# Modulation product on TensorE inside the RWKV and attention turns, and a down projection split into high and low parts

## What is computed

```python
# first block, 256 tokens, D = 2048, D_FF = 5632
def hybrid_mixer(h, ...):                   # attention: 12 heads, RWKV: 12 heads of 64
    z = h @ w_in
    ...
    return jnp.concatenate([oa, ob, oc], axis=-1) @ w_out
def conv_ffn(h, w_up, conv_w, conv_b, w_down):
    up = h @ w_up                           # 2048 x 11264
    ...                                     # causal convolution of width 3
    return (jax.nn.gelu(gate, approximate=True) * val) @ w_down      # 5632 x 2048
# second block, two layers, on x and on a context ctx
for l in range(DEPTH_2):
    sh_l, sc_l, g_l = jnp.split(jax.nn.silu(c) @ w_mod[l] + b_mod[l], 3, axis=-1)      # w_mod[l]: 2048 x 6144
    sh_c, sc_c, g_c = jnp.split(jax.nn.silu(c_ctx) @ w_mod[l] + b_mod[l], 3, axis=-1)
    hl = xl * (1.0 + sc_l[:, None, :]) + sh_l[:, None, :]
    hc = xc * (1.0 + sc_c) + sh_c
    ...
```

## Time and profile before

| what | us |
|---|---|
| runs before: median (lowest, highest) | 3780.88 (3779.40, 3785.93) |
| span of the profiled execution | 3779.2 |
| PE busy in the span | 3340.1 (88%) |
| DVE busy | 1918.9 (51%) |
| ACT busy | 1163.8 (31%) |
| one RWKV turn (six of them) | 81.93 |
| attention, six turns | 60.51 |
| up projection, from its opening to its last matmul | 495.62 |
| from there to the last matmul of down | 308.00 |
| from there to the first matmul of the second block | 50.36 |

### The profile page before, as it was taken

The page is one execution under the profiler, slowest core; times in us unless marked ns, Lnnn a source line. Parts: engine busy times, 40 slices in busy tenths (PEclk is TensorE's granted clock), DMA queues, the critical chain, the costliest instruction groups (busy, mean ns, idle before and its releaser), DMA issues.

```text
span 3779.2 us, 47105 instructions
## 1 busy us (share of the span) xinstructions
PE 3340.1 (88%) x18040; PEld 2719.8 (72%) x18040; DVE 1918.9 (51%) x2906; ACT 1163.8 (31%) x1744; POOL 67.8 (2%) x129
## 2 busy tenths in 40 slices
PE   7988888589679999999959999999987969998977
PEld 6876666489579999988836864444446848887877
DVE  4444444455269999977762212222234354246565
ACT  3321111354345555400011223222231223245542
POOL 0000000000000000000000000000000000000000
PEclk8999998699789999999979999999998979999989
DMA  7411111134237777788852221111112204233332
GB/s 218 167 56 55 44 55 44 72 104 162 99 115 274 269 270 277 266 305 312 316 198 106 95 90 56 55 55 56 67 67 100 100 34 145 100 124 110 112 134 100
DMA packets 73108, 508.70 MB, mean 135 GB/s; under 512 B 8332, under 2 KB 8460, under 8 KB 19664
## 3 DMA queue, kind: packets, MB, share of 16 engines
q1 hardware_dynamic: 55440, 377.00, 28.0%
q0 software_dynamic: 17600, 130.75, 9.4%
HBM read 496.97 MB, written 10.75 MB: 134 GB/s over the span
## 4 chain that ended last, share of the span: by engine, by line
PE 73%; DVE 12%; DMA 7%; issue 4%; ACT 3%; DVEq 0%; ACTq 0%; SPq 0%; POOLq 0%
PE bank L544 37%; PE bank L840 10%; DMA y_f<-in_w_mod 5%; PE bank L845 5%; PE bank L596 3%; PE bank L638 2%; PE bank L495 2%; DVE x_f L1610 2%; PE bank L874 2%; PE bank L513 2%; DVE x_f L1262 1%; DVE ring_f32r L1262 1%; DMA ring_f<-in_w_in 1%; PE bank L888 1%; DVE x_f L1750 1%
## 5 line engine op out<-in xcount | busy, mean ns | idle before, releaser
L544 PE MATMUL bank<-y_f32r,high_f32r 128*128 128x256 f32 (+1 forms) x3312 | 1029.6, 311 | 56.5 <-DVE h_f32r L1262 30.2
L1262 DVE TENSOR_TENSOR ring_f32r<-ring_f,high_f32r 128x1024 fp32r<-128x1024 f32 x494 | 588.8, 1220 | 667.0 <-ACT high_f32r L946 666.4
L544 PE MATMUL bank<-y_f32r,ring_f32r 128*128 128x256 f32 (+1 forms) x2608 | 803.6, 308 | 0.0
L544 PE MATMUL bank<-h_f32r,high_f32r 128*128 128x256 f32 (+1 forms) x2432 | 743.0, 305 | 1.9 <-DVE ring_f32r L1262 1.9
L946 ACT CAST high_f32r<-ring_f 128x1024 fp32r<-128x1024 f32 x494 | 491.9, 1045 | 733.5 <-PE bank L544 609.5
L544 PEld LDWEIGHTS bank<-y_f32r,high_f32r 128*128 128x128 f32 x3312 | 636.5, 192 | 91.6 <-issue 48.0
L544 PEld LDWEIGHTS bank<-y_f32r,ring_f32r 128*128 128x128 f32 x2608 | 503.1, 193 | 22.3
L544 PEld LDWEIGHTS bank<-h_f32r,high_f32r 128*128 128x128 f32 x2432 | 468.0, 192 | 21.3 <-DVE ring_f32r L1262 2.7
L1610 DVE SCALAR_TENSOR_TENSOR x_f<-y_f,h_f 128x2048 f32<-128x2048 f32 x192 | 439.4, 2289 | 85.8 <-DMA y_f<-in_w_mod 82.1
L840 PE MATMUL bank<-h_f,ring_f 128*128 128x512 f32 x1024 | 457.2, 597 | 0.0
L840 PEld LDWEIGHTS bank<-h_f,ring_f 128*128 128x128 f32 x1024 | 194.2, 192 | 215.3 <-issue 213.2
(11 more groups left out here) (336 smaller groups left out, 3749.8 us busy)
## 6 DMA issues: line engine op xcount, KB each, us to landing
ring_f<-in_w_in SPq DMA_DIRECT2D x159, 1024.0 KB, 4.8
y_f<-in_w_mod POOLq DMA_DIRECT2D x96, 1024.0 KB, 6.6
ring_f<-in_w_up SPq DMA_DIRECT2D x88, 1024.0 KB, 4.8
ring_f<-in_w_out SPq DMA_DIRECT2D x48, 1024.0 KB, 4.8
ring_f<-in_w_down SPq DMA_DIRECT2D x64, 704.0 KB, 5.9
ring_f<-in_w_kv SPq DMA_DIRECT2D x8, 1024.0 KB, 4.8
ring_f<-in_w_q SPq DMA_DIRECT2D x4, 1024.0 KB, 4.8
ring_f<-in_w_o SPq DMA_DIRECT2D x4, 1024.0 KB, 4.8
```

Source lines behind the costliest of these rows:

```text
L544: last = mm(bk[(t0 + j) % banks][:, 0:width], w[:, c], x[:, k], start=(k == 0 and w is hi and x is rhs.hi), stop=(k == KC - 1 and w is lo))
L1262: return v.tensor_tensor(out, in0, in1, op)
```

## The change

Part one moves the modulation from DVE to TensorE. silu(c) and silu(c_ctx) are two columns of a stationary operand of 32 columns (`mod_c`, the other 30 are zero); the weights are the moving operand, 512 columns wide. A group of 512 outputs takes 16 such matmuls in sequence, four in each of four ring slabs (`mod_slab`), into partitions 0 to 31 of a bank. ACT copies the row out (`mod_row`), and four small matmuls turn it into 4 x 2 columns (`mod_turned`), which ACT copies into MOD. There are 24 groups: three in each RWKV turn, handed out by `projection1` as pieces (a slab is a piece, a turning is one), and one in each attention turn. The weights now come through the ring, on SP. A turn of RWKV loads 16 slabs where it loaded four.

Part two gives the down projection the three float32r passes of `gemm3`: ACT splits each slab of weights and, in three parts, the gated activations; DVE makes the low parts. The squares of its output are summed tile by tile (`down_sum`) and not at the end.

```diff
+MOD_TURN = 3
+TURN = [("mod", 0), ("in1", 0), ("turned", 0), ("mod", 1), ("in1", 1), ("turned", 1), ("mod", 2), ("in1", 2), ("turned", 2),
+        ("in1", 3)]
...
+            def mod_slab(at_slot, bank, q, c=mod_c):
+                for m in range(4):
+                    last = mm(bank[0:32, :], c[:, 4 * q + m, :], at_slot[:, m * 512:(m + 1) * 512],
+                              start=(q == 0 and m == 0), stop=(q == 3 and m == 3))
+                last.then_inc(gemm_done if q == 3 else S("mod_read"), 1)
+            def mod_turned(bank, row=mod_row):
+                for m in range(4):
+                    last = mm(bank[:, 2 * m:2 * m + 2], row[0:32, m * P:(m + 1) * P], mod_sel[0:32, :], start=True, stop=True)
+                last.then_inc(gemm_done, 1)
...
-                beside1(8)
+                beside1(3)
                 pe.wait_ge(S("rw_kksq"), i + 1)
...
-                beside1(20)
+                beside1(18)
                 pe.wait_ge(S("rw_ops"), i + 1)
...
-                beside1(12)
+                beside1(8)
                 pe.wait_ge(S("rw_bonus"), i + 1)
...
                 def evacuated(dve, act=None):
-                    beside1(1)
+                    beside1(2)
...
-                beside1(1)
+                beside1(3)
                 pe.wait_ge(S("rw_w0"), i + 1)
...
+                    beside1(1)
                     pe.wait_ge(S("ch_U"), i * 4 + (c + 1))
...
+                    beside1(1)
...
-                beside1(9)
+                beside1(16)
...
-                    for k in range(DOWN):
-                        last = mm(bk[(TILE0["down"] + j) % 2][:, 0:T], slot[s % SLOTS][:, k * P:(k + 1) * P],
-                                  Z[:, q * DOWN + k, :], start=(q == 0 and k == 0), stop=(q == 3 and k == DOWN - 1))
+                        for m, (w, x) in enumerate(((w_hi[p % 2], hi), (w_hi[p % 2], act_lo[:, kk, :]), (w_lo[s % SLOTS], hi))):
+                            last = mm(bk[t % 2][:, 0:T], w[:, c], x, start=(kk == 0 and m == 0), stop=(kk == FT - 1 and m == 2))
...
-            colsum(H[0], KC, T, "down")
+            down_sum(15, stop=True)
...
@@ ACT, in an RWKV turn
-                beside1(0, i)
-                beside1(1, i)
+                for n in range(4):
+                    beside1(n, i)
                 for n, (dst, b) in enumerate(((m_p2t, 3), (m_p4t, 3), (m_p2, 2))):
...
-                beside1(2, i)
+                for n in range(4, 7):
+                    beside1(n, i)
                 act.wait_ge(S("rw_turned"), i + 1)
...
@@ DVE, behind the up loop
-            with dve.Fori(0, 26) as i:
-                for u in range(2):
-                    for c in range(2):
-                        modulation(u, c, i, 22)
+            with dve.Fori(0, 7) as i:
+                for k in range(8):
+                    low("down", 4 + k, i)
...
             dve.wait_ge(S("ctx_loaded"), 16)
+            dve.wait_ge(S("down_used"), 3 * 15 + 2)
```

More of the change, by code:

```diff
@@ L200, in __init__ @@
                 self.hi_f = self.hi.bitcast(F32)
-        kbase = whole.take(2 * P)
-        ident, ones = kbase[:, 0:P], kbase[:, P:2 * P]
+        kbase = whole.take(2 * P + 2)
+        ident, ones, mod_sel = kbase[:, 0:P], kbase[:, P:2 * P], kbase[:, 2 * P:2 * P + 2]
         vecs = whole.take(NV)
@@ L444, in _ @@
             load(x_all[:, KC * T:], d["memT"], "mem_loaded")
[L446 to L456, removed]
+            pool.wait_ge(rhs_made, RHS0["kv"] + 4)
             load(x_all[:, KC * T:], d["ctxT"], "ctx_loaded")
@@ L943, in high @@
                 s, p = SLAB0[name] + t, SPLIT0[name] + t
-                act.wait_ge(w_in_slot[s % SLOTS], (i + (s // SLOTS + 1)) * 16)
-                for half in (slice(0, SLOT // 2), slice(SLOT // 2, SLOT)):
+                n, turn = (DOWN * P, 2) if name == "down" else (SLOT, 1)
+                act.wait_ge(w_in_slot[s % SLOTS], (i * turn + (s // SLOTS + 1)) * 16)
+                for half in (slice(0, n // 2), slice(n // 2, n)):
                     act.copy(w_hi[p % 2][:, half], slot[s % SLOTS][:, half]).then_inc(w_high, 1)
@@ L1146, in up, with act_highs @@
                 if j % 2:
                     act.wait_ge(gemm_free, i * 4 + (TILE0["up"] + j))
-                    f(gl[j // 2], cv[j - 1], ACT.Gelu_apprx_tanh).then_inc(S("f_gelu"), 1)
-            turns(act, 84, up)
-            for j in range(4):
-                up(j, 21, ahead=(j < 2))
-            evac("down", lambda t: at(Y[0], t), squares=H[0], ahead=False)
+                    f(gl[j % 4 // 2], cv[j % 4 - 1], ACT.Gelu_apprx_tanh).then_inc(S("f_gelu"), 1)
+            def act_highs(part):
+                t0, n = ACT_FIRST[part], (ACT_FIRST[part + 1] - ACT_FIRST[part]) // 2
+                act.wait_ge(S("f_act"), ACT_FIRST[part + 1] + 1)
+                for m in range(2):
+                    act.copy(act_hi[part][:, m * n:(m + 1) * n], Z[:, t0 + m * n:t0 + (m + 1) * n]).then_inc(S("act_high"), 1)
@@ new lines, in _ @@
+            for part, (first, last) in enumerate(((0, 8), (8, 16))):
+                with act.Fori(0, last - first - 1) as i:
+                    for j in range(4):
+                        up(4 * first + j, i)
+                for j in range(4):
+                    up(4 * last - 4 + j, 0)
+                    if j == 1 and part:
+                        act_highs(0)
+            with act.Fori(0, 5) as i:
+                for j in range(4):
+                    up(64 + j, i)
+            for j in range(4):
+                up(84 + j, 0, ("up", 2) if j < 2 else ("down", -86))
+                if j == 1:
+                    act_highs(1)
@@ new lines, in _, with down @@
+            act_highs(2)
+            def down(j, i, ahead=True):
+                for q in range(4):
+                    k = 4 * j + q
+                    if q < 3:
+                        act.wait_ge(S("down_used"), i * 6 + (3 * j + q + 1))
+                    else:
+                        act.wait_ge(gemm_done, i * 2 + (TILE0["down"] + j + 1))
+                    if ahead or q < 2:
+                        high("down", k + 2, i)
+                b = bk[(TILE0["down"] + j) % 2][:, 0:T]
+                act.copy(at(Y[0], i * 2 + j), b)
+                if j >= 2:
+                    act.wait_ge(S("down_summed"), i * 2 + (j - 1))
+                f(down_sq[:, j % 2, :], b, ACT.Square).then_inc(gemm_free, 1)
@@ L1154, in _ @@
+            down(0, 0)
+            down(1, 0)
+            with act.Fori(0, 6) as i:
+                down(2, i)
+                down(3, i)
+            down(14, 0)
+            down(15, 0, False)
             root()
@@ L1368, in _ @@
             v.memset(lora[0], 0.0)
+            v.memset(mod_c, 0.0)
             step(v.memset(lora[1], 0.0))
```

271 lines of the change are left out of this document (197 added, 74 removed).

## The result

| | us |
|---|---|
| kernel before, in the same runs: median (lowest, highest) | 3780.14 (3775.71, 3785.93) |
| kernel after: median (lowest, highest) | 3970.76 (3967.97, 3973.19) |
| ratio, with its 95% interval | 1.0498 (1.0485 to 1.0512) |
| span of the profiled execution after | 3971.4 |

The change costs 191 us.

What follows compares the result with a forecast made beforehand. TensorE, 73% of the span, was taken to set the pace. From 3779.2 us, RWKV +205, attention +59, sums behind it -3, silu +2.5, down -45, behind down -42 gave 3955.7, plus 1.7: 3957 us, range 3912 to 4008.

Steps and rivals of the forecast that it cites:

- A slab at 3.44 us: Modulation on TensorE: a slab's four narrow matmuls cost the full-width 3.44 us, upper end 3.94; 96 slabs are 330 us.
- the path terms: RWKV turn, added time: norm +6.9, products +2.7, inverse start +9.5, seventh wait +3.1, eighth +6.1, ninth +4.0 us.
- +34.2: Growth of one RWKV turn in us, 36.6 + 2.6 - 5; over six turns +205 us.
- The clock in a turn: RWKV turn: TensorE stays at 2.4 GHz, giving back about 5 us of 13.66 at half speed (0 to 6.8).
- the switches: RWKV turn: 17 switches of matmul width at some 0.15 us each, +2.6 us a turn.
- Attention: Six attention turns grow from 10.1 to 19.9 us each, +59 us (50 to 71); +56 with the sums behind them.
- The credit of 3: Sums behind attention: attention ends at full clock, so they take 3 us less.
- Down and behind it: Down in float32r takes 263.1 for 308.0, -45 us (-48 to -35); the gap behind it 8.7 for 50.4, -42.
- Half clock under narrow work: Rival: work on a quarter of the array does not keep the clock up, slabs take 6.9 us, total 4285 us; 5%.
- The split as the bound of down: Rival: ACT's waits and tile copies make a down slab 4.9 us, not 3.96; down 60 us longer, total 4017; 4%.
- More hidden than counted: Rival: an RWKV turn takes 104 us, +22, with attention at its lower end, total 3872 us; 5%.
- Overlap of narrow matmuls: Rival: consecutive matmuls on 32 columns run side by side, a slab costs 0.86 us, total 3711 us; 6%.

Runs made afterwards that it cites:

- quarter slab: The changed kernel with only the first of each slab's four matmuls, all loads, copies and turnings kept: 3754.6 us, 0.9931 of the kernel before.
- the first experiment: The changed kernel with each slab's four matmuls written to four groups of 32 partitions and summed by the turning: 3747.8 us, 0.9914 of the kernel before.

## Why the prediction was right, and where its sizes were off

- **A slab at 3.44 us:** held, 3.47 in groups and 3.55 alone. The quarter slab shows that this carries the whole loss: without three quarters of it the change is 216 us faster.
- **RWKV, the path terms**, each against the full-clock price that the forecast used: norm 10.42 - 3.46 = +6.96 (forecast +6.9); products 448.99 - 437.36 - 8.66 = +2.97 (+2.7); start of the inverse 469.21 - 453.53 - 5.99 = +9.69 (+9.5); from there to the seventh wait's end 21.95 for 18.97, +2.98 (+3.1); eighth and ninth 15.37 for 5.22, +10.15 (+10.1). Twelve changes at 0.13 are in these already; the forecast had 17 at 0.15 beside them, +2.6. A short turn came out at +33.4 for +34.2.

  But the norm's 3.46 was not what the kernel before paid there. It ran at 1.2 GHz from 432.78 to 436.19, and its eight pieces took 4.39 us (434.31 to 438.70). Counted from the turn's start the norm comes only 12.35 - 6.98 = 5.37 us later. Before, then after:

```profile
431.72:438.70 6.98, 6.98 (x25) 5.81 (x26) 3.62 (x11) 3.67 (x5) 0.00 (x0) 0.76 0.26 109
```

```profile
424.38:436.73 12.35, 12.35 (x33) 3.99 (x33) 1.23 (x3) 3.63 (x5) 0.00 (x0) 1.00 0.58 202
```

- **The clock in a turn is the term that was mis-sized.** The forecast took it to stay at 2.4 GHz once pieces fill the chunk loop, worth -5 in every turn. In the loop it did. These are the chunk loop and the matmuls behind it, before, then after:

```profile
487.87:500.15 12.28, 8.76 (x32) 6.04 (x32) 2.84 (x10) 0.00 (x0) 0.00 (x0) 0.62 0.00 0
500.15:503.13 2.98, 2.98 (x20) 2.47 (x20) 0.56 (x2) 0.00 (x0) 0.00 (x0) 0.50 0.00 0
```

```profile
514.23:524.50 10.27, 10.14 (x49) 6.11 (x49) 3.35 (x12) 0.00 (x0) 0.00 (x0) 1.00 0.00 0
524.50:526.11 1.61, 1.61 (x19) 1.39 (x19) 0.06 (x1) 0.00 (x0) 0.00 (x0) 1.00 0.00 0
```

  They gave back 2.0 and 1.4, with eight pieces in the loop at no cost; three pieces behind those, which the kernel before ran at 1.2 GHz until 504.46, gave 0.6, and the turn's start, which the forecast had missed, 1.6. That is 5.6. But the changed turn has half clock of its own, 3.4 us in a short one and 13.6 in a long one. That of the short turn lies here, and costs 1.6:

```profile
506.53:514.23 7.70, 7.70 (x34) 5.75 (x34) 0.85 (x2) 0.37 (x1) 0.00 (x0) 0.78 0.28 119
```

  So the clock gave a short turn about 4.0 of the 5, and cost a long one about 0.9, being 4.9 longer. The three long turns came out at +38.2 for the forecast's +34.2; these 12 us are the 11 by which the stage exceeds +205. In the short turns what the clock lacked, 1.0, was covered by the switches, 1.6 for the 2.6 forecast.

- **Attention, +55.8 for +56, with two errors that cancel.** The turns grew by 56.2 (118.76 for 62.60; forecast 59, a turn being 19.0 and not 19.9). The clock behind them did rise, 0.93 for 0.78, and the 52 matmuls of the sums took 2.8 us less; but the stretch lasted 21.03 for 21.37, since DVE's chain is what ends it. The credit of 3 was given back as waiting.
- **Output projection to up, +6.4 for 0.** Not foreseen. The instructions are the same; the trace has 66.0 us at 1.2 GHz in this stage before and 78.3 after. Half of the difference is 6.2 of the 6.4 us, were PE at work in all of it. Its plainest piece is a column sum that lasted 6.79 us at full clock. Before, then after:

```profile
885.13:891.92 6.79, 6.79 (x32) 5.99 (x33) 0.74 (x1) 0.00 (x0) 0.00 (x0) 1.00 0.20 84
```

```profile
1158.22:1168.01 9.79, 9.79 (x32) 8.10 (x33) 0.74 (x1) 0.00 (x0) 0.00 (x0) 0.69 0.14 58
```

  Every variant shows +2.0 to +6.5 here, also those with four tiles. Why the clock falls there in some and not in others stays open.
- **Down and behind it, -43.1 and -41.4 for -45 and -42.** PE set the pace (261 of 264.8 us busy). The split didn't, and up lost nothing to the activations' split.
- **The rivals.** Half clock under narrow work: no, 0.97 in attention. The split as the bound of down: no. More hidden than counted, a turn of 104: no, the shortest is 115.35. Overlap of narrow matmuls: not in the change, as argued from its one group of partitions; in the first experiment, yes.

  The trace of the kernel before could have told more than the earlier trace rows. In spatial gating, 16 matmuls with 64 stationary columns write the lower and the upper half of the partitions in turn, two matmuls with two sums to a half (`o = 64 * (g % 2)`):

```profile
696.73 3.74 PE L736 MATMUL bank<-y_f 128*64 128x128 f32 x32 [1.16 <-ACT y_f L1056]
```

```profile
696.73:700.50 3.77, 3.74 (x32) 3.34 (x32) 0.00 (x0) 1.66 (x2) 0.00 (x0) 0.50 0.02 4
```

  At 458.23 in the earlier trace rows, 16 full-width records of 128 moving columns take 2.05 us at 2.4 GHz. The 32 records here would take about 8 us by that at 1.2 GHz, and took 3.74: two halves make it twice as fast, and their four sums do not make it more, so that in the first experiment, too, the four groups of partitions are the likely cause and not the four sums. No run separates the two for 32 columns.

## What to carry to other kernels

Before work is moved to a fuller engine, price it there and ask what it frees: here 330 us of TensorE bought 35 us behind down, since in up VectorE had been hidden anyway. A narrow stationary operand cost the full price while all its matmuls wrote one group of partitions (3.47 us a slab, 3.43 with 128 columns); spread over four groups, the same matmuls took about a quarter of the time, and a loss of 5.0% became a gain of 0.9%. Before such work is priced, look for narrow matmuls in the trace that already write more than one group. Then look at the ring: a faster piece needs its loads earlier, and a tile that is handed out in pieces keeps its slot from the loads that the next burst needs. And count what the other engines take back when a wait goes: here 10 of 14 us.

## What was not expected of the hardware

- The same program of the RWKV turns ran in 88.1 to 89.7 us a turn in one kernel and in 91.7 to 93.7 in another (turns two to five), with 50.3 and 63.5 us of the stage at 1.2 GHz. In the change itself, turns of equal code alternate between 115.35 and 120.23.
- A change between 32 and 128 stationary columns cost 0.12 to 0.20 us where it could be read alone, 0.13 on average. The Trainium skill (TensorEngine Tiling (Array Packing), Key Properties) says that a change of mode drains the engine; the trace agrees and gives it this price.
